# Sparse attention: the selection mask joins VectorE's first pass instead of a matmul, and scores are made three units ahead instead of two

## The reference

```python
_, idx = lax.top_k(score, k_sel)
c_sel = jax.vmap(lambda c, i: c[i])(c_kv, idx)
dist = tq[None, :, None] - idx
bias = jnp.moveaxis(rel_bias[relative_bucket(dist)], -1, 2)
logits = jnp.einsum('bqhc,bqkc->bqhk', qa, c_sel) * (DSA_DH ** -0.5)
logits = jnp.where((dist >= 0)[:, :, None, :], logits + bias, -1e30)
p = jax.nn.softmax(logits, axis=-1).astype(c_sel.dtype)
return jnp.einsum('bqhk,bqkc->bqhc', p, c_sel)
```

## Time and profile before

| what | value |
|---|---|
| median of 3 runs | 3671.53 us (3669.49 to 3679.2) |
| profiled execution, its own time | 3675.04 us |
| its span | 3673.3 us |
| granted TensorE clock, mean of the span | 0.962 |
| busy over the span: TensorE, VectorE, ScalarE, GpSimd | 92%, 49%, 33%, 29% |
| `sparse_stage`, from the first scores to ScalarE's last copy | 390.4 to 655.4 us |

### The profile page before, as it was taken

The page is one execution under the profiler, slowest core; times in us unless marked ns, Lnnn a source line. Parts: engine busy times, 40 slices in busy tenths (PEclk is TensorE's granted clock), DMA queues, the critical chain, the costliest instruction groups (busy, mean ns, idle before and its releaser), DMA issues. The chain is left out here.

```text
span 3673.3 us, 47286 instructions
## 1 busy us (share of the span) xinstructions
PE 3374.9 (92%) x18438; PEld 2663.1 (73%) x18438; DVE 1797.0 (49%) x3327; ACT 1207.5 (33%) x2253; POOL 1069.2 (29%) x588
## 2 busy tenths in 40 slices
PE   7699899589999999999999989999898999998988
PEld 5378666489878877888888867777566677775667
DVE  1687677755454534645455571234444412335443
ACT  3366455434322222000000041334454112344540
POOL 2123000055244535344353523220111333201112
PEclk9799999699899999999999999999999999999999
DMA  3111100000211113323132212110102212101011
GB/s 116 30 35 35 32 5 1 1 8 1 92 45 57 54 41 101 102 67 105 57 101 71 63 29 98 43 50 12 20 5 74 82 35 64 46 18 17 8 70 69
DMA packets 234300, 179.91 MB, mean 49 GB/s; under 512 B 42944, under 2 KB 219248, under 8 KB 233216
## 3 DMA queue, kind: packets, MB, share of 16 engines
q1 hardware_dynamic: 230944, 176.53, 15.7%
q10 hardware_dynamic: 3168, 0.81, 0.1%
HBM read 159.92 MB, written 16.87 MB: 48 GB/s over the span
## 5 line engine op out<-in xcount | busy, mean ns | idle before, releaser
L1146 DVE SCALAR_TENSOR_TENSOR y_T<-y_T 128x1024 f32<-128x1024 f32 x48 | 137.4, 2914 | 0.1
L925 ACT ACTIVATE I-13676a_hi<-I-13675act_f 128x512 fp32r<-128x512 f32 x22 | 13.5, 633 | 338.5 <-DVE I-13675act_f L934 338.5
L958 DVE TENSOR_TENSOR x_T<-x_T,I-13682p_d 128x512 f32<-128x512 f32 x88 | 60.3, 687 | 126.2 <-PE I-13682p_d L890 126.2
L283 PE MATMUL I-13680p_g<-hf_hi,I-13656w_hi 128*128 128x512 f32 x352 | 108.8, 390 | 3.4 <-POOL hf_lo L523 3.4
L283 PE MATMUL I-13681p_u<-hf_hi,I-13657w_hi 128*128 128x512 f32 x352 | 109.1, 391 | 2.3 <-POOL I-13659w_lo L269 2.3
L1732 DVE TENSOR_TENSOR I-22736S<-I-22736S,c_causal 128x256 f32<-128x256 f32 x32 | 13.8, 431 | 198.5 <-PE I-22736S L1659 198.5
L285 PE MATMUL I-13681p_u<-hf_lo,I-13657w_hi 128*128 128x512 f32 x352 | 109.1, 391 | 0.0
L287 PE MATMUL I-13681p_u<-hf_hi,I-13659w_lo 128*128 128x512 f32 x352 | 108.8, 390 | 0.0
L287 PE MATMUL I-13680p_g<-hf_hi,I-13658w_lo 128*128 128x512 f32 x352 | 108.4, 389 | 0.0
L285 PE MATMUL I-13680p_g<-hf_lo,I-13656w_hi 128*128 128x512 f32 x352 | 108.4, 389 | 0.0
L1732 DVE TENSOR_TENSOR I-16421S<-I-16421S,c_causal 128x256 f32<-128x256 f32 x32 | 13.8, 431 | 192.0 <-PE I-16421S L1659 192.0
(11 more groups left out here) (1396 smaller groups left out, 10209.6 us busy)
## 6 DMA issues: line engine op xcount, KB each, us to landing
y_T<-in_w_ada SPq DMA_DIRECT2D x48, 512.0 KB, 3.5
saved_x<-x_T SPq DMA_DIRECT2D x3, 4096.0 KB, 13.7
I-13654w_raw<-in_w_gate SPq DMA_DIRECT2D x22, 512.0 KB, 4.5
I-13655w_raw<-in_w_up SPq DMA_DIRECT2D x22, 512.0 KB, 4.1
...
```

What stands on the lines that cost most here:

```text
L283: nc.tensor.matmul(out[h], w_hi[:, k, :], hi(k, h), start=(k == 0), stop=False)
L925: nc.scalar.activation(a_hi[s][:, cols], act_f[:, cols], ACT.Copy).then_inc(a_rounded, 1)
L958: nc.vector.tensor_tensor(x_n, x_n, p_d[n % 2][:, h, :], ALU.add).then_inc(d_added[n % 2], 1)
L1146: self.nc.vector.scalar_tensor_tensor(out=self.raw[s], in0=self.raw[s], scalar=1.0, in1=self.c_row, op0=ALU.mult, op1=ALU.mult, accum_out= ...
```

## The change

The mask is no longer added by TensorE. VectorE's first pass (L2712 now) adds it while it reads the scores from PSUM, in one instruction that also takes the row minimum and moves the sums to `probs`. For that, scores and mask change sign: the absorbed queries are scaled by -1/8, the flipped identity is negated, and the masks are written as +2^100 by `index_stage`. The third pass then reads only SBUF (`part` and `moved`) and not `S`. `S` is free after the first pass (`reduced`), and TensorE makes the scores of unit u+3 where it made those of u+2. The exponent's bias takes two small instructions, of which the second waits for the first. ScalarE waits for the third pass ahead of both exponentials; before, the first of them needed only `grid` and the bias.

```diff
@@ index_stage, VectorE
-                    own(v.tensor_copy(masks(t), scores(t)))
+                    own(v.tensor_scalar(masks(t), scores(t), -1.0, None, ALU.mult))
...
-                    own(v.tensor_scalar(masks(t), scores(t), 0.0, MASKED, ALU.is_gt, ALU.mult))
+                    own(v.tensor_scalar(masks(t), scores(t), 0.0, -MASKED, ALU.is_gt, ALU.mult))
@@ sparse_stage, TensorE
                     if u > 1:
-                        pe.wait_ge(rest_done, u - 1)
+                        pe.wait_ge(reduced, u - 1)
...
-                        mm(out_u[:, h, 0:b - a], q, c_T[:, a:b], start=True, stop=False)
+                        last = mm(out_u[:, h, 0:b - a], q, c_T[:, a:b], start=True, stop=(b <= (t - 1) * P))
...
-                        last = mm(out_u[:, h, 0:b - a], unit_b[:, :], mask(t)[:, a:b], start=False, stop=True)
...
-                scores(0)
-                scores(1)
+                for u in range(3):
+                    scores(u)
                 for u in range(UNITS):
-                    if u + 2 < UNITS:
-                        scores(u + 2)
+                    if u + 3 < UNITS:
+                        scores(u + 3)
                     turn(u)
@@ ScalarE
-                    act.wait_ge(gridded, u + 1)
+                    act.wait_ge(rest_done, u + 1)
                     act.wait_ge(bias_set, u + 1)
-                    nc.scalar.activation(part[:, 0:w], part[:, 0:w], ACT.Exp, bias=neg[:, u % 4:u % 4 + 1])
-                    act.wait_ge(rest_done, u + 1)
-                    nc.scalar.activation(rest[:, 0:w], rest[:, 0:w], ACT.Exp, scale=-1.0).then_inc(exp_done, 1)
+                    nc.scalar.activation(part[:, 0:w], part[:, 0:w], ACT.Exp, bias=neg[:, u % 4:u % 4 + 1], scale=-1.0)
+                    nc.scalar.activation(rest[:, 0:w], rest[:, 0:w], ACT.Exp).then_inc(exp_done, 1)
@@ VectorE, to_grid_of
-                    v.tensor_scalar(shift, src, GRID_ROUND, TAKEN, ALU.add, ALU.max, accum_out=top[:, one]).then_inc(shifted, 1)
-                    dve.wait_ge(shifted, u + 1)
-                    v.tensor_scalar(part, shift, GRID_ROUND, GRID / 2, ALU.subtract, ALU.add).then_inc(gridded, 1)
-                    v.tensor_scalar(neg[:, one], top[:, one], GRID_ROUND, -1.0, ALU.subtract, ALU.mult).then_inc(bias_set, 1)
+                    v.tensor_tensor_reduce(out=moved, in0=src, in1=mask(unit(u)[2]), scale=1.0, scalar=-TAKEN, op0=ALU.add, op1=ALU.min,
+                                           accum_out=least[:, one]).then_inc(reduced, 1)
+                    dve.wait_ge(reduced, u + 1)
+                    v.tensor_scalar(part, moved, GRID_ROUND, GRID_ROUND, ALU.add, ALU.subtract).then_inc(gridded, 1)
+                    v.tensor_scalar(least[:, one], least[:, one], GRID_ROUND, None, ALU.add).then_inc(least_shifted, 1)
+                    dve.wait_ge(least_shifted, u + 1)
+                    v.tensor_scalar(neg[:, one], least[:, one], GRID_ROUND, GRID / 2, ALU.subtract, ALU.add).then_inc(bias_set, 1)
                     dve.wait_ge(gridded, u + 1)
-                    v.scalar_tensor_tensor(out=shift, in0=shift, scalar=GRID_ROUND, in1=src, op0=ALU.subtract, op1=ALU.subtract).then_inc(rest_done, 1)
+                    v.tensor_tensor(moved, part, moved, ALU.subtract).then_inc(rest_done, 1)
```

19 lines of the change are left out of this document (9 added, 10 removed).

## The result

| what | before | changed |
|---|---|---|
| median | 3670.86 us (4 runs) | 3646.38 us (4 runs, 3643.69 to 3648.2) |
| ratio to before | | 0.9923, 95% interval 0.9909 to 0.9936 |
| profiled execution, its own time | 3675.04 us | 3643.69 us |
| its span | 3673.3 us | 3641.9 us |
| `sparse_stage`, first scores to last copy | 264.9 us | 244.5 us |

The change makes the kernel 0.8% faster: 24.5 us by the medians, where 18 were forecast. The direction and what bounds the stage were right, the size was too small. 3646.38 us lies in the band of rival A (3642 to 3648), though what A says didn't happen: the two waits at the start of a pair are still there. In the stage 20.4 us were gained; the rest, 4 us by the medians and 11 by the two profiled executions, lies outside it.

What follows compares the result with a forecast made beforehand. TensorE was taken as the bound, busy 244.66 of the stage's 265 us. Savings of 3 x 2.6 + 3 x 2.4 + 2 x 1.5 = 18 us gave 3653 us, range 3643 to 3662; the forecast's own band, 3648 to 3659, had 0.60.

Steps and rivals of the forecast that it cites:

- rival A: Start-of-pair passes: TensorE's waits vanish too, leaving only its own work, 28.3 us; 25.6 us saved, 3646 us; chance 0.17.
- The mask matmuls: TensorE, sparse stage: removing 4608 mask columns a pass saves 2.0 us each, 15.8 us over eight passes.
- The operations' prices: VectorE: first and third passes change at no cost; the second small instruction adds 0.15 us, 10 us in 64 units.
- C: VectorE's first pass: the bf16 mask slows it to a scan's pace, 38 us more; 3671 us, no change; chance 0.05.
- D: VectorE's third pass: two SBUF inputs run at the feed-forward subtraction's pace, 99 us more; 3718 us; chance 0.04.
- The walk through a pass that begins a pair: Timed steps from VectorE's first pass over the 1024 unit: 13.6 + 16.85 = 30.5 us instead of 33.1, 2.6 less.
- its scores ended 0.2 us earlier: Start-of-pair pass: the 1024 unit's scores end 0.2 us before VectorE's first pass over it, which is time 0.
- loses its 2.0 us of masks and most of 0.5 us of idle time: Mid-pair passes, where TensorE is the bound before and after: 2.4 us saved in each of three.
- TensorE without a pause: Start-of-pair pass behind the 896 unit's transposes: 20.6 us of unbroken TensorE work, shrinking to 16.85.
- where the same sum gives 28.4: Pass that begins the last pair: 28.4 us instead of 31.0, 2.6 less.
- Rival B: Start-of-pair chain: the look-ahead gives nothing and the chain grows 0.45 us; 7.3 us saved, 3664 us; chance 0.14.
- The ends: First and last passes of the stage: each saves between nothing and 2.6 us, taken as 1.5.

Runs made afterwards that it cites:

- filled: Changed kernel with ScalarE's 256-unit aux copy behind the 1024 unit's exponentials, one small bias instruction, and two absorbed-query steps moved to a pair's last and first units: 3641.26 us.
- before_three_ahead: Kernel before, mask matmuls kept, with scores made three units ahead and S still freed by the third pass: 3662.79 us, ratio 0.9972.
- before_no_mask: Kernel before without the mask matmuls, so every key is attended to, scores still two units ahead: 3663.0 us, ratio 0.9968.
- two_ahead: Changed kernel with scores made two units ahead again, mask still in VectorE's first pass: 3663.46 us, ratio 0.9972.
- act_reordered: Changed kernel with ScalarE's aux copy of the 256 unit moved behind the exponentials of the 1024 unit: 3646.99 us, ratio 0.9928.
- late_free: Changed kernel with scores waiting for VectorE's third pass again instead of the first: 3645.79 us, ratio 0.9921; run again, 3651.69 us, ratio 0.9935.
- delayed: Changed kernel with 17 extra subtractions of 1024 columns on VectorE at the sparse stage's end: 3668.01 us, ratio 0.9986.

## Why the prediction was right in kind and short in size

**What bounds the stage: right.** TensorE busy 228.2 us (229 forecast), VectorE 206.7. `filled`, which puts work of the same stage where TensorE waited, shows it most directly.

**The mask matmuls: the price was right, 2.0 us a pass, 15.8 in all.** `before_three_ahead` and the changed kernel have no bracket at a turn in a mid-pair pass, and differ there by 32.04 - 30.04 = 2.00 us. The 14.1 us by which the listed busy time falls in `before_no_mask` are fewer because new waits hide in it, as the one at its 128 unit. Alone the missing matmuls shorten the stage by 10.4.

**The operations' prices: right.** First pass 1.23 us, third 1.22, the extra small instruction 0.14 (0.15 forecast). Rivals C and D are out, the first by the first pass's own row, the second by the third pass's. The shorter third pass that the Trainium skill, "VectorE: DVE Perf Modes", section "The TRN2 errata", would have (65 ns less, an estimate from its cycles) didn't come: 1.22 us with both inputs in SBUF here, as for L2719 with one in PSUM.

**The walk through a pass that begins a pair: right to 0.1 us, by two errors that cancel.** ScalarE's aux copy came 4.86 us after the first pass over the 1024 unit (5.4 forecast), the exponentials ended at 7.6 (8.0), the transposes were at 8.89 (9.35) and 13.15 (13.6), the wait 1.84 (2), the rest 17.23 (16.85), the pass 30.38 (30.5). Each of the first four is 0.4 to 0.5 us early for the same reason: the step "its scores ended 0.2 us earlier" failed. The first pass started 452.18 - 451.55 = 0.63 us behind the scores, since it waited for the turn of unit u-3, which frees `probs`. That later zero makes the part behind it look longer by as much. That the aux copy sets the exponentials is shown by `act_reordered`. Rival A needed both waits gone; they shrank from 2.83 to 2.15 us in sum.

**The step that failed: listed busy time was taken for work.** In the prediction's words a mid-pair pass "loses its 2.0 us of masks and most of 0.5 us of idle time", and the part of a pass that is "TensorE without a pause" was carried over to the last pair, "where the same sum gives 28.4". Mid-pair passes gained 2.78 us, not 2.4: the 2.00 of masks, and 0.78 that the look-ahead took, of which 0.67 was the one wait at the turn of the 1024 unit that the bracket gives as 0.51. Where the other 0.1 lay is not shown. The start of the last pair gained 3.4, not 2.6. Its part behind the 896 unit's transposes wasn't free of pauses: in before the turns of the 512 and 384 units waited there, the first like this:

```profile
643.30 0.28 PE L2595 MATMUL I-2920S<-x_T,I-2900unit_b 128*128 128x256 bf16 x1
643.82 0.66 PE L2608 MATMUL I-2922PT<-c_ident,I-2908probs 128*128 128x128 f32 x4 [0.23 <-DVE I-2908probs L2724]
```

Start to start 0.52 us instead of 0.12, and 0.25 instead of 0.07 at the 384 unit: 0.58 us, of which brackets show 0.23. With the look-ahead both are gone. These two kinds of pass make 1.15 and 0.8 us; with 0.25 at the other starts and 0.2 at the ends that is the 2.4 us between 18 and 20.4.

The sums agree. TensorE's listed busy time fell from 244.66 to 228.24 us and its idle time from 20.3 to 16.3. Of the 16.4 us of busy time 15.8 are masks; the changed kernel's slower clock in the drain (below) puts 0.9 back, so some 1.5 us were waits listed as busy. `two_ahead` shows the same, with the changed kernel's 1356 matmuls: 231.78 us busy against 228.24. In a mid-pair pass the twelve bias matmuls of 256 columns take 4.30 and 3.19 us there, start of each to start of the next matmul; brackets show 0.78 of the 1.1 between them.

**The look-ahead's own worth: underrated.** I had it as moving work around a chain. Before the experiment I expected 2 to 6 us from it alone; `before_three_ahead` shows 10.4, half of the gain, and without it the missing masks bring 10.4, not 15.8. Rival B, that it gives nothing, is out. B's 7.3 us are close to the 7.5 of `two_ahead`, but that is luck: B has mid-pair passes gain 1.6 us and starts of a pair 0.5, and there they gain 1.1 each. Of its two parts the earlier release of `S` is worth nothing measurable (`late_free`), since TensorE then waits a few matmuls earlier inside the same 4.26 us.

**The ends: 3 us forecast, 3.2 measured**, but nearly all at the first pass. In the drain the changed kernel's profile has TensorE at a clock of 0.96 in the last window: two matmuls took 1.97 us there, and 1.07 in the profile before. `late_free` and `delayed`, at 1.00, end the same drain 0.9 us sooner (34.74 and 34.75 us after the first pass over the last 1024 unit, against 35.62), so 21.3 us would be the gain at an equal clock.

**Outside the stage: a term that the sum did not have.** By the medians 24.5 - 20.4 = 4 us come from there, by the two profiled executions 11. Some 1.5 us lie right behind the stage and came in both profiles of either kernel; 4.9 lie in the attention layer, where TensorE did the same matmuls at a lower clock in before. The prediction took 18 us off the profiled execution and left all other stages as they were. Over the kernels run here the surplus is 0.9 to 7.4 us, and none in `delayed`. That the change brings the clock about is not shown. The surplus is of the size of one such outcome.
